# A two-block decoder kernel: three projections in products of 512 columns instead of 256

## The chip, the cores and the metric

The kernel runs on one core of one Trainium2 chip. The metric is the device time of one execution in microseconds, and the time of a kernel is the median over its runs. TensorE multiplies, VectorE, ScalarE and GpSimd work on tiles, SyncE issues the transfers of the weights; they meet over semaphores.

## The reference, cut to what matters

Two decoder blocks follow each other, each on 256 tokens of 2048 features. All of it is float32.

```python
# first block (three mixers, then)
merged = (sigmoid(g_a) * (y_a @ wb[:r_a]) + sigmoid(g_b) * (y_b @ wb[r_a:r_b])
          + sigmoid(g_c) * (y_c @ wb[r_b:]))
x = x + merged @ w_out                                  # the first output projection, "wout"
x = x + conv_ffn(rms_norm(x, ffn_norm), ffn_w_up, ffn_conv_w, ffn_conv_b, ffn_w_down)
x = rms_norm(x, final_norm)
# second block
z = rms_norm_2(x, mix_norm_gain) @ w_in
h = x + concatenate([pool_mixer(z...), mla(z...)]) @ w_out_2
xn = rms_norm_2(h, ffn_norm_gain)
q = (xn @ w_pq).reshape(B, S, 8, 2, 128)                # the query projection, "pq"
s1, s2 = q[..., 0, :] @ sub_k1.T, q[..., 1, :] @ sub_k2.T
# top 16 of each, top 16 of their sums, softmax: gates of 128 experts a token out of 16384
h = h + sum_k gelu(expert_u[idx] . xn) * gate * expert_v[idx]
gate = sigmoid(rms_norm_2(h, ple_norm_gain) @ w_ple_gate)   # the last gate, "pg"
h = h + gate * (p @ w_ple_proj)
```

## The kernel before, in words

**Layout.** Activations lie transposed: feature tile k (128 features) is a tile of 128 partitions by 256 tokens, and 16 such tiles, k = 0 to 15, make the 2048 features. Weights come as panels of 128 x 2048 (1 MB): panel n holds, for one tile of output features, the 16 blocks of 128 x 128 that meet the 16 input tiles. SyncE fills a ring of two slots with the panels in one fixed order, in four quarters of four blocks each (fill and refill, L587). A quarter of a split panel is refilled when its low part has been taken.

**Split products.** To keep float32 accuracy with the faster 32-bit matmul type, each operand is cut into a high and a low part. ScalarE writes the high part of each quarter of a panel into whi (high_quarter, L472), after TensorE has read the same quarter of the panel before it: the fourth quarter waits for panel_done. VectorE (quarters 1 and 3) and GpSimd (quarters 0 and 2) subtract and write the low part, wlo (rests, L485; rest_one, L568; rests_alone, L493). There is one whi and one wlo, so the preparation follows one quarter behind the products. Activations are split alike; high and low part of the normalised input lie side by side in xhl, and those of the merged tiles in mhl, each 16 tiles high and then 16 tiles low.

**Two forms of a block.** In the narrow form (project_split and products, L659 to L661) block k of a panel is three products of 256 columns: high weights by high input, high weights by low input, low weights by high input, all summed in one half of a bank of PSUM:

```python
                pe.matmul(out, whi[:, b], hi, start=start, stop=False, **kw)
                pe.matmul(out, whi[:, b], lo, start=False, stop=False, **kw)
                return pe.matmul(out, wlo[:, b], hi, start=False, stop=stop, **kw)
```

In the wide form (project_wide, L694 and L695) the high weights meet both input parts in one product of 512 columns, whose second half lands in the second half of the bank, and the low weights follow with 256 columns. Whoever reads the bank adds its halves. Before the change, the wide form stands in the feed-forward up projection (88 panels) and in the expert panels from number 36 on (92 panels); the narrow form in wout, in the second block's input projection, in wout2, pq, pg and the first 36 expert panels. The down projection and the expert outputs use a third form (L775 to L777).

**Evacuation.** Panel p goes to bank p mod 4 and waits until the panel four before has been evacuated (evac_done). The evacuation is VectorE's in all places that the change touches:

- wout: evac_add takes the rests of the next panel, waits for panel_done, and adds the bank to the residual (L1301 is the helper's line). ScalarE's high_and_squares waits for that, writes the high tile of the next input (tile_high, L546), after each fourth panel squares four tiles (L2152), and only then goes on to the high parts of the panel after next. VectorE writes the low tile (tile_low, L552). GpSimd folds the squares (fold, L562) between its rests. The first up panel reads the tiles as they come; in the second one TensorE sums the folded squares (folded_sums, L747), from which VectorE makes rstd (statistics: L1304 and the reciprocal L1318, with ScalarE's root between).
- pq: query(j) multiplies the bank by rstd into q2, normal(j) (L1307) writes tile j of the expert input. Panels 0 and 1 are evacuated only after the statistics, and no rest of VectorE is placed between them. After the last ones come the residual parts of the expert input (x_rest, L576) and query(15); the score products (L1251) wait for all 16 queries, ScalarE copies them out, and VectorE's top-16 code, the digits of the indices and GpSimd's 256 indirect transfers (L2768, the scatter of the gates) follow while TensorE does the expert panels.
- pg: gate(j) takes the rests of the next panel, waits for panel_done and multiplies the bank by rstd into gx; ScalarE (embed) applies the sigmoid and then makes the high parts of the panel after next; finish(j) multiplies with the projected embedding and adds to the residual. SyncE writes the output in four pieces as finish goes on.

The order on each engine is written out by hand; the class Count numbers the steps on a semaphore, link makes the engine wait for its own instruction, and enter and leave carry the count through loops. VectorE's add_residual and the last gate run as hardware loops of four panels a turn.

## Time and profile before

| | us |
|---|---|
| median of 3 runs | 3664.87 |
| lowest and highest | 3664.02, 3666.03 |
| the profiled execution, its own time | 3666.28 |
| its span | 3664.70 |
| granted TensorE clock, mean share of full speed | 0.992 |

The page gives busy times of each engine, the chain that ended last and the costliest groups. Where it ends, the timeline of an engine in a short stretch shows each instruction with its start, its length, and, in brackets, the idle time before it with the one that released it. Products overlap in the records: a product's length runs until its end is out of the array, while the next one has begun. wout runs from about 816 to 911 us, up from 911, pq from 2001 to 2097, the scores to 2110, pg from 3562 to 3659.

### The profile page before, as it was taken

How to read it: one execution, taken by the hardware profiler on the slowest of the kernel's cores; microseconds unless marked ns; L12 is line 12 of the kernel's file. 1: busy time of each engine (PE TensorE's matmuls, PEld its weight loads, DVE VectorE, ACT ScalarE, POOL GpSimd, SP SyncE). 2: the span in 40 equal slices, each digit the busy share in tenths (PEclk: the TensorE clock that was granted, in tenths of full speed). 3: DMA queues.
4: the chain of work that ended last, by engine and by line, in shares of the span. 5: the costliest groups of instructions: out<-in, count | busy, mean ns of one | idle time of the engine just before them, and what ended most of it. 6: DMA issues, size and time to landing. Idle time of an engine off the chain costs nothing.

```text
span 3664.7 us, 69606 instructions
## 1 busy us (share of the span) xinstructions
PE 3589.7 (98%) x21612; PEld 3174.8 (87%) x21612; DVE 2128.0 (58%) x3499; ACT 1771.0 (48%) x3033; POOL 1846.1 (50%) x1326
## 2 busy tenths in 40 slices
PE   8999999999999999998999999999999999999999
PEld 6889989999888888888869999988888888888889
DVE  6759764555777775336446597655555433333345
ACT  1134455545444444555335456554554555555554
POOL 0005665555555554444135483777776455555543
PEclk9999999999999999999999999999999999999999
DMA  5444444565677765664424555777777776776655
GB/s 175 144 142 154 155 152 135 175 201 179 210 231 231 232 198 181 193 193 136 132 94 160 174 185 183 184 186 187 187 185 183 228 215 218 218 216 215 217 187 166
DMA packets 388742, 672.38 MB, mean 183 GB/s; under 512 B 75968, under 2 KB 76096, under 8 KB 386064
## 3 DMA queue, kind: packets, MB, share of 16 engines
q1 hardware_dynamic: 344304, 630.48, 55.2%
q0 software_dynamic: 44320, 40.32, 5.2%
q8 instruction: 74, 1.21, 0.1%
q14 instruction: 44, 0.36, 0.0%
HBM read 649.53 MB, written 21.10 MB: 183 GB/s over the span
## 4 chain that ended last, share of the span: by engine, by line
PE 71%; POOL 13%; issue 6%; DVE 6%; ACT 2%; DMA 1%; SPq 0%; ACTq 0%; POOLq 0%; DVEq 0%; PEldq 0%
POOL gates L2768 11%; PE ps L694 9%; PE ps L775 8%; PE ps L776 8%; PE ps L777 8%; PE ps L659 8%; PE ps L661 7%; PE ps L660 7%; PE ps L648 5%; PE ps L695 4%; DVE arena L1301 2%; POOL wlo L493 1%; PE ps L1077 1%; DMA gates<-arena 1%; ACT arena L2152 1%
## 5 line engine op out<-in xcount | busy, mean ns | idle before, releaser
L472 ACT ACTIVATE whi<-ring 128x512 fp32r<-128x512 f32 x2180 | 1356.0, 631 | 1284.5 <-PE ps L661 441.9
L485 POOL TENSOR_TENSOR wlo<-ring,whi 128x512 fp32r<-128x512 f32 x714 | 964.3, 1352 | 1037.7 <-ACT whi L472 1037.1
L485 DVE TENSOR_TENSOR wlo<-ring,whi 128x512 fp32r<-128x512 f32 x702 | 568.8, 816 | 841.7 <-ACT whi L472 821.9
L694 PE MATMUL ps<-xhl,whi 128*128 128x512 f32 x2880 | 1019.2, 399 | 9.4 <-DVE wlo L493 6.6
L695 PE MATMUL ps<-xhl,wlo 128*128 128x256 f32 x2880 | 806.9, 280 | 0.0
L659 PE MATMUL ps<-xhl,whi 128*128 128x256 f32 x2320 | 666.3, 287 | 16.8 <-DVE wlo L485 4.7
L694 PEld LDWEIGHTS ps<-xhl,whi 128*128 128x128 f32 x2880 | 541.6, 188 | 147.5 <-DVE wlo L485 9.0
L660 PE MATMUL ps<-xhl,whi 128*128 128x256 f32 x2320 | 659.3, 284 | 0.0
L661 PE MATMUL ps<-xhl,wlo 128*128 128x256 f32 x2320 | 659.2, 284 | 0.0
L695 PEld LDWEIGHTS ps<-xhl,wlo 128*128 128x128 f32 x2880 | 544.3, 189 | 0.0
L775 PE MATMUL ps<-whi,xhl 128*128 128x512 f32 x1360 | 529.1, 389 | 0.0
L776 PE MATMUL ps<-wlo,xhl 128*128 128x512 f32 x1360 | 529.1, 389 | 0.0
L777 PE MATMUL ps<-whi,xhl 128*128 128x512 f32 x1360 | 529.1, 389 | 0.0
L2768 POOL DMA_INDIRECT gates<-arena x256 | 412.1, 1610 | 188.8 <-issue 93.4
L659 PEld LDWEIGHTS ps<-xhl,whi 128*128 128x128 f32 x2320 | 447.8, 193 | 21.8 <-issue 5.5
L660 PEld LDWEIGHTS ps<-xhl,whi 128*128 128x128 f32 x2320 | 448.1, 193 | 0.2
L661 PEld LDWEIGHTS ps<-xhl,wlo 128*128 128x128 f32 x2320 | 447.8, 193 | 0.0
L493 DVE TENSOR_TENSOR wlo<-ring,whi 128x512 fp32r<-128x512 f32 x384 | 258.2, 697 | 226.5 <-ACT whi L472 226.4
L775 PEld LDWEIGHTS ps<-whi,xhl 128*128 128x128 f32 x1360 | 255.3, 188 | 53.2 <-POOL wlo L485 0.2
L776 PEld LDWEIGHTS ps<-wlo,xhl 128*128 128x128 f32 x1360 | 255.3, 188 | 53.0
L777 PEld LDWEIGHTS ps<-whi,xhl 128*128 128x128 f32 x1360 | 255.3, 188 | 52.8
L493 POOL TENSOR_TENSOR wlo<-ring,whi 128x512 fp32r<-128x512 f32 x176 | 236.8, 1370 | 107.2 <-ACT whi L472 103.2
(259 smaller groups left out, 4096.7 us busy)
## 6 DMA issues: line engine op xcount, KB each, us to landing
ring<-stream SPq DMA_DIRECT2D x2380, 256.0 KB, 3.6
gates<-arena POOLq DMA_DIRECT2D x16, 1024.0 KB, 6.6
arena<-gates POOLq DMA_DIRECT2D x32, 512.0 KB, 6.3
gates<-arena POOLq DMA_INDIRECT x256
res<-xT SPq DMA_DIRECT2D x4, 512.0 KB, 8.1
res<-xT POOLq DMA_DIRECT2D x1, 2048.0 KB, 11.2
outT<-res POOLq DMA_DIRECT2D x1, 2048.0 KB, 9.6
parked<-outT POOLq DMA_DIRECT2D x1, 2048.0 KB, 11.1
```

The source lines that it names most:

```text
L472: act.activation(quarters(whi, g), quarters(ring[:, n % SLOTS, :], g), ACT.Copy).then_inc(w_hi, 1)
L485: eng.tensor_tensor(quarters(wlo, g), quarters(ring[:, n % SLOTS, :], g), quarters(whi, g).bitcast(F32), ALU.subtract).then_inc(done, 1)
L493: eng.tensor_tensor(quarters(wlo, g), quarters(ring[:, n % SLOTS, :], g), quarters(whi, g).bitcast(F32), ALU.subtract).then_inc((w_lo_pool ...
L659: pe.matmul(out, whi[:, b], hi, start=start, stop=False, **kw)
L660: pe.matmul(out, whi[:, b], lo, start=False, stop=False, **kw)
L661: return pe.matmul(out, wlo[:, b], hi, start=False, stop=stop, **kw)
L694: pe.matmul(ps[:, p % 4, :], whi[:, b], xhl[:, :, t], start=(k == 0), stop=False, skip_group_check=True)
L695: mm = pe.matmul(ps[:, p % 4, 0:T], wlo[:, b], xhi[:, t], start=False, stop=(k == KD - 1), skip_group_check=True)
L775: pe.matmul(ps[:, 4 * b + g, :], hi, whi[:, w], start=first, stop=False)
L776: pe.matmul(ps[:, 4 * b + g, :], hi, wlo[:, w], start=False, stop=False)
L777: mm = pe.matmul(ps[:, 4 * b + g, :], lo, whi[:, w], start=False, stop=end)
L2768: pool.indirect_dma_start(gates, bass.IndirectOffsetOnAxis(ap=place[:, c:c + 1], axis=0), weight[:, c:c + 1], None, compute_op=ALU.add).th ...
```

## The change

TensorE does wout, pq and pg in the wide form. project_wide gets the waits for the parts of its input and the choice of the input (xhl, or mhl for the merged tiles); residual_wide takes the place of split_residual, and wide_loop that of split_loop in pq and pg. VectorE brings the halves together: in wout by a second addition to the residual, in pq and pg by a reduction of the bank into half a free bank (6 and 5), which the multiplication by rstd then reads. The first addition and the reductions are steps of their own (L), so the counts of the loops change with them.

```diff
--- before.py
+++ after.py
@@ -681,18 +681,20 @@
                     if middle and g == 1:
                         middle()
 
-            def project_wide(n, p, i=None, tiles=None, middle=None):
+            def project_wide(n, p, i=None, tiles=None, middle=None, name=None, x=xhl):
 
 
                 pe.wait_ge(evac_done, turn(i, 4, p - 3))
                 for g in range(4):
                     quarter_ready(n, g, i, 4)
+                    if name:
+                        pe.wait_ge((x_lo_pool, x_lo_dve)[g % 2], XQ[name] // 2 + g // 2 + 1)
                     for k in range(4 * g, 4 * g + 4):
                         b, t = slice(k * P, (k + 1) * P), slice(k * T, (k + 1) * T)
                         if tiles:
                             pe.wait_ge(t_lo, TILES[tiles] + k + 1)
-                        pe.matmul(ps[:, p % 4, :], whi[:, b], xhl[:, :, t], start=(k == 0), stop=False, skip_group_check=True)
-                        mm = pe.matmul(ps[:, p % 4, 0:T], wlo[:, b], xhi[:, t], start=False, stop=(k == KD - 1),
+                        pe.matmul(ps[:, p % 4, :], whi[:, b], x[:, :, t], start=(k == 0), stop=False, skip_group_check=True)
+                        mm = pe.matmul(ps[:, p % 4, 0:T], wlo[:, b], x[:, 0, t], start=False, stop=(k == KD - 1),
                                        skip_group_check=True)
                     mm.then_inc(quarter_used if g < 3 else panel_done, 1)
                     if middle and g == 1:
@@ -747,14 +749,22 @@
                     mm = pe.matmul(ps[:, bank, 0:T], ones, sq[:, k * T:(k + 1) * T], start=(k == 0), stop=(k == 3))
                 mm.then_inc(rms_ss, 1)
 
-            def split_residual(n, p, name, r, sq):
-
-                x = parts_of(name)
+            def residual_wide(n, p, name, x):
+
                 for j in range(4):
-                    project_split(n + j, p + j, name if j == 0 else None, x=x)
+                    project_wide(n + j, p + j, name=name if j == 0 else None, x=x)
                 with pe.Fori(0, 3) as i:
                     for j in range(4, 8):
-                        project_split(n + j, p + j, None, i, x=x)
+                        project_wide(n + j, p + j, i, x=x)
+
+            def wide_loop(n, p, count):
+
+                turns = count // 4
+                with pe.Fori(0, turns) as i:
+                    for j in range(4):
+                        project_wide(n + j, p + j, i)
+                for j in range(4 * turns, count):
+                    project_wide(n + j, p + j)
 
             def accumulate_all(n, count, tiles_before, p_end, first_tile, last_read):
 
@@ -1036,7 +1046,7 @@
             with pe.Fori(0, 3) as i:
                 for m in range(4, 8):
                     merge(m, i)
-            split_residual(PANELS["wout"], OUT["wout"], "merged", 1, nx())
+            residual_wide(PANELS["wout"], OUT["wout"], "merged", mhl.rearrange("p (a t) -> p a t", a=2))
 
 
             project_wide(PANELS["up"], OUT["up"], tiles="ffn")
@@ -1236,9 +1246,9 @@
                     half_panel(j, g)
 
 
-            project_split(PANELS["pq"], OUT["pq"], None, tiles="ffn2")
-            project_split(PANELS["pq"] + 1, OUT["pq"] + 1, None, middle=lambda: folded_sums(6, sq_attn))
-            split_loop(PANELS["pq"] + 2, OUT["pq"] + 2, KD - 2)
+            project_wide(PANELS["pq"], OUT["pq"], tiles="ffn2")
+            project_wide(PANELS["pq"] + 1, OUT["pq"] + 1, middle=lambda: folded_sums(6, sq_attn))
+            wide_loop(PANELS["pq"] + 2, OUT["pq"] + 2, KD - 2)
             n = PANELS["subk"]
             arrive(n)
             for b in range(2):
@@ -1277,11 +1287,11 @@
                 mm.then_inc(panel_done, 1)
 
             pe.wait_ge(S["pp_ev"], 1)
-            project_split(PANELS["pg"], OUT["pg"], None, tiles="ple")
+            project_wide(PANELS["pg"], OUT["pg"], tiles="ple")
             pe.wait_ge(S["pp_ev"], 3)
-            project_split(PANELS["pg"] + 1, OUT["pg"] + 1, None, middle=lambda: folded_sums(7, nx()))
+            project_wide(PANELS["pg"] + 1, OUT["pg"] + 1, middle=lambda: folded_sums(7, nx()))
             pe.wait_ge(S["pp_ev"], 7)
-            split_loop(PANELS["pg"] + 2, OUT["pg"] + 2, KD - 2)
+            wide_loop(PANELS["pg"] + 2, OUT["pg"] + 2, KD - 2)
 
 
         @block.vector
@@ -1347,9 +1357,11 @@
                     one(j)
                 with dve.Fori(0, count // 4 - 1) as i:
                     evac.enter(i, 4)
+                    step.enter(i, 4)
                     for j in range(4, 8):
                         one(j, i)
                     evac.leave(count // 4 - 1)
+                    step.leave(count // 4 - 1)
                 tile_low(dve, name, count - 1)
 
             def evac_add(p, j, i=None):
@@ -1357,7 +1369,8 @@
                 rests(dve, n + 1, i, 4)
                 dve.wait_ge(panel_done, turn(i, 4, n + 1))
                 c = res[:, j * T:(j + 1) * T] if i is None else res[:, bass.ds(i * (4 * T) + j * T, T)]
-                evac.link(tt(c, c, ps[:, p % 4, 0:T], ALU.add))
+                L(tt(c, c, ps[:, p % 4, 0:T], ALU.add))
+                evac.link(tt(c, c, ps[:, p % 4, T:2 * T], ALU.add))
 
             def panel_of(p):
 
@@ -1938,10 +1951,15 @@
             statistics(6, meanwhile=lambda: rests(dve, PANELS["pq"] + 2))
             evac.base, evac.k = OUT["pq"], 0
 
+            def both_halves(out, bank):
+
+                return dve.tensor_reduce(out, ps[:, bank, :].rearrange("p (a t) -> p t a", a=2), AX.X, ALU.add)
+
             def query(j):
 
                 dve.wait_ge(panel_done, PANELS["pq"] + j + 1)
-                evac.link(tt(q2[:, j * T:(j + 1) * T], ps[:, (OUT["pq"] + j) % 4, 0:T], rstd[:], ALU.mult))
+                L(both_halves(ps[:, 6, 0:T], (OUT["pq"] + j) % 4))
+                evac.link(tt(q2[:, j * T:(j + 1) * T], ps[:, 6, 0:T], rstd[:], ALU.mult))
 
             def normal(k):
 
@@ -2105,7 +2123,8 @@
                 dve.wait_ge(panel_done, turn(i, 4, PANELS["pg"] + j + 1))
                 if j >= 2:
                     dve.wait_ge(S["gate_act"], turn(i, 4, j - 1))
-                evac.link(tt(gx[j % 2], ps[:, j % 4, 0:T], rstd[:], ALU.mult))
+                L(both_halves(ps[:, 5, 0:T], j % 4))
+                evac.link(tt(gx[j % 2], ps[:, 5, 0:T], rstd[:], ALU.mult))
 
             def finish(j, i=None):
 
@@ -2123,8 +2142,8 @@
                 gate(j)
                 finish(j - 1)
             with dve.Fori(0, KD // 4 - 2) as i:
-                for c in (step, evac, N["out_ready"]):
-                    c.enter(i, 4)
+                for c, per in ((step, 8), (evac, 4), (N["out_ready"], 4)):
+                    c.enter(i, per)
                 for j in range(4, 8):
                     gate(j, i)
                     finish(j - 1, i)
```

## Rows read from the trace of the kernel before

**Rows 1.** The page, part 1: busy time, share of the span and instructions of each engine.

```profile
PE 3589.7 (98%) x21612; PEld 3174.8 (87%) x21612; DVE 2128.0 (58%) x3499; ACT 1771.0 (48%) x3033; POOL 1846.1 (50%) x1326
```

**Rows 2.** The page, part 4: the chain that ended last, by engine and by line.

```profile
PE 71%; POOL 13%; issue 6%; DVE 6%; ACT 2%; DMA 1%; SPq 0%; ACTq 0%; POOLq 0%; DVEq 0%; PEldq 0%
POOL gates L2768 11%; PE ps L694 9%; PE ps L775 8%; PE ps L776 8%; PE ps L777 8%; PE ps L659 8%; PE ps L661 7%; PE ps L660 7%; PE ps L648 5%; PE ps L695 4%; DVE arena L1301 2%; POOL wlo L493 1%; PE ps L1077 1%; DMA gates<-arena 1%; ACT arena L2152 1%
```

**Rows 3.** Timeline of TensorE where the scatter ends: start, length, instruction, [idle, releaser].

```profile
2840.77 0.79 PE L694 MATMUL ps<-xhl,whi 128*128 128x512 f32 x1 [6.56 <-DVE wlo L493]
```

**Rows 4.** The page, part 5: groups of products, mean ns of one.

```profile
L694 PE MATMUL ps<-xhl,whi 128*128 128x512 f32 x2880 | 1019.2, 399 | 9.4 <-DVE wlo L493 6.6
...
L659 PE MATMUL ps<-xhl,whi 128*128 128x256 f32 x2320 | 666.3, 287 | 16.8 <-DVE wlo L485 4.7
```

**Rows 5.** Busy time by window, L659, then L694: stretch, length, PE busy (count), PEld, clock.

```profile
2024.00:2096.00 72.00, 56.60 (x200) 38.40 (x201) 1.00 0.64 188
...
2500.00:2700.00 200.00, 200.00 (x567) 106.36 (x566) 1.00 0.77 185
```

**Rows 6.** Timeline of the first output projection, panels 3 to 5.

```profile
841.68 0.41 DVE L1301 TENSOR_TENSOR res<-res,ps 128x256 f32<-128x256 f32 x1
...
844.33 1.67 ACT L472 ACTIVATE whi<-ring 128x512 fp32r<-128x512 f32 x3 [0.55 <-ACT arena L2152]
...
845.04 2.99 POOL L485 TENSOR_TENSOR wlo<-ring,whi 128x512 fp32r<-128x512 f32 x2 [4.07 <-ACT whi L472]
...
845.52 3.06 DVE L485 TENSOR_TENSOR wlo<-ring,whi 128x512 fp32r<-128x512 f32 x2 [2.90 <-ACT whi L472]
...
846.38 0.39 PE L659 MATMUL ps<-mhl,whi 128*128 128x256 f32 x1 [0.26 <-POOL wlo L485]
```

**Rows 7.** Groups of the up projection by form, 1000 to 1050 us.

```profile
L1701 DVE TENSOR_REDUCE ps<-ps 128x256 f32<-128x512 f32 x9 | 6.2, 686 | 0.0
```

**Rows 8.** Timeline of the hand-over from first output projection to up.

```profile
915.76 1.29 POOL L568 TENSOR_TENSOR wlo<-ring,whi 128x512 fp32r<-128x512 f32 x1 [3.76 <-ACT whi L472]
...
917.19 0.47 PE L694 MATMUL ps<-xhl,whi 128*128 128x512 f32 x1
```

**Rows 9.** Timeline of the first output projection, ahead of panel 10.

```profile
871.54 2.85 POOL L562 TENSOR_TENSOR arena<-arena 128x1024 f32<-128x1024 f32 x1
...
873.11 1.14 ACT L472 ACTIVATE whi<-ring 128x512 fp32r<-128x512 f32 x2
```

**Rows 10.** Timeline of the query projection, panels 1 to 3.

```profile
2008.51 0.36 PE L659 MATMUL ps<-xhl,whi 128*128 128x256 f32 x1 [0.82 <-POOL wlo L485]
...
2018.72 1.75 DVE L1318 RECIPROCAL rstd<-rstd 128x256 f32<-128x256 f32 x1 [1.04 <-ACT rstd L2152]
...
2022.81 1.28 DVE L485 TENSOR_TENSOR wlo<-ring,whi 128x512 fp32r<-128x512 f32 x2
...
2023.55 0.39 PE L659 MATMUL ps<-xhl,whi 128*128 128x256 f32 x1
```

**Rows 11.** Timeline where the query projection ends and the scores begin.

```profile
2099.86 0.35 PE L1251 MATMUL ps<-ring,arena 128*128 128x128 f32 x1 [2.62 <-DVE arena L1301]
```

**Rows 12.** Timeline of the last gate, panels 0 to 4.

```profile
3584.21 1.28 ACT L2152 ACT_TABLE_LOAD   x1
...
3587.84 2.19 ACT L472 ACTIVATE whi<-ring 128x512 fp32r<-128x512 f32 x4
...
3589.89 0.38 PE L659 MATMUL ps<-xhl,whi 128*128 128x256 f32 x1 [0.67 <-POOL wlo L485]
```

**Rows 13.** Timeline of the last gate's loop, ScalarE and GpSimd.

```profile
3609.79 1.18 ACT L472 ACTIVATE whi<-ring 128x512 fp32r<-128x512 f32 x2
...
3610.49 1.29 POOL L485 TENSOR_TENSOR wlo<-ring,whi 128x512 fp32r<-128x512 f32 x1 [2.48 <-ACT whi L472]
...
3615.96 1.15 ACT L472 ACTIVATE whi<-ring 128x512 fp32r<-128x512 f32 x2 [0.53 <-ACT arena L2152]
```

**Rows 14.** Timeline of VectorE, its last evacuation.

```profile
3659.34 0.43 DVE L1301 TENSOR_TENSOR arena<-ps,rstd 128x256 f32<-128x256 f32 x1 [3.14 <-PE ps L661]
```

## Prediction

> **What bounds the kernel now.** I read the page's engine table first, then the chain that ended last, then the costliest groups, then panels in order of time. TensorE is busy 98% of the span [rows 1], and the chain runs through its products for most of the time, except for 11% on GpSimd's scatter of the gates [rows 2]. That scatter is started by VectorE after the query projection and ends in a TensorE wait of 6.56 us [rows 3]; work before it and after it adds up in one line, so a stage's shift is a shift of the end. One panel is 16 blocks k. A block is three products of 256 columns in the narrow form and one of 512 plus one of 256 in the wide form. The busy sums of the groups (287 ns and 399 ns a product [rows 4]) overlap and must not be added: they would promise 176 ns a block. What counts is how many blocks go by. In a narrow stretch without a wait 200 blocks take 72 us, 0.360 us each; in a wide stretch 567 take 200 us, 0.353 us each [rows 5]. Both forms push 768 columns through a block, which is why the two are so near.
>
> **Products, 48 panels.** The change takes 768 blocks from 0.360 to 0.353 us. That is 0.007 us a block, 0.112 us a panel and 5.4 us in all if TensorE never waited. It waits, so below each stage is followed to the point where something else sets its pace.
>
> The Trainium skill (TensorE: Matmul & The Clock Gate, Back-to-back issue gap) gives a warm gap of N/2.4 ns plus about 2.5 ns a product. By it one product fewer a block would save 2.5 ns, 1.9 us in all, an estimate; the rows show nearly three times that, and the sum goes by the rows. The same section also names a sustained 131 ns for products of 512 columns; rows 5 leave no room for it, since a wide block would then be far shorter than 0.353 us.
>
> **VectorE, new work.** In the first output projection evac_add becomes two linked additions. One takes 0.41 us [rows 6]; with the link the second costs 0.45 us. In the other two stages a reduction from 512 to 256 goes ahead of the multiplication: the feed-forward stage has this very operation at 0.686 us [rows 7], with the link 0.73 us. VectorE has room for both, since it is busy 58% of the span [rows 1]. So the new work costs nothing where nobody waits for the evacuation soon. The bound is 0.45 or 0.73 us for each place where somebody does, and zero elsewhere. The places:
>
> **First output projection (wout).** Each fourth panel, ScalarE squares four tiles after the evacuation before it makes the high parts of the panel after next. The chain is addition at 841.68, high tile and squares, high parts at 844.33, GpSimd's rest at 845.04, restart of TensorE at 846.38 after a wait [rows 6]. There is no slack in it, so the second addition goes in whole. This occurs at panels 5, 9 and 13 of the stage and once more in the hand-over to the first up panel, where GpSimd's rest at 915.76 releases the product at 917.19 [rows 8]. Ahead of panels 10 and 14 a fold on GpSimd from 871.54 to 874.39 holds its next rest, while the first of two high parts (873.11, 1.14 for both) is ready about 0.65 us sooner [rows 9]; 0.45 us more is hidden there, but what TensorE gains in panels 9 and 13 is lost. Sum: panel 0 gives three quarters (its second quarter waits for VectorE), 0.084, and panels 1 to 3 0.336; then +0.45 leaves +0.03. Panels 5 to 7 give 0.336, +0.45: +0.14. Panels 10 and 11 give 0.224, +0.45: +0.37. Panels 14 and 15 give 0.224, +0.45: **+0.6 us** for the stage. In the other panels GpSimd's rest is ready about 1.2 us before it is needed, and 0.45 + 0.11 fits.
>
> **Query projection (pq).** Panel 0 gains nothing, since panel 1 starts behind a GpSimd rest that TensorE does not drive (2008.51) [rows 10]. Then comes a knot: after the reciprocal (2018.72) VectorE does query 0, normal 0, query 1, normal 1, and only at 2022.81 the rest that panel 3's second quarter waits for; TensorE restarts at 2023.55 [rows 10]. Both queries get 0.73 us longer, +1.46, less the 0.112 of panel 1 that the reciprocal follows: +1.35. From there 12.75 panels without a wait give back 1.43. At the tail VectorE goes from query 14 over normals and residual parts to query 15 without a pause, and the score products wait 2.62 us for it, until 2099.86 [rows 11]. Both are longer again, +1.46, from a TensorE that is at +0.03 at the end of panel 14: **+1.5 us**. TopK, the scatter and the expert panels all start from there and shift alike.
>
> **Last gate (pg).** Panels 0 and 1 are held by folds and squares that do not depend on products. The evacuations 0 and 1 run ahead of and under ScalarE's table load, which ends at 3585.49 and which the first sigmoid waits for [rows 12], so their 1.46 us are hidden: if that cover were gone they would cost at most that. Gate 2 is not: it leads to the sigmoid, the high parts at 3587.84 and TensorE's restart at 3589.89 [rows 12]. +0.73 less 0.056: +0.67. Twelve panels give 1.34. In each of them the same chain is there with slack: high parts at 3609.79 and GpSimd's rest at 3610.49 for 1.29 us [rows 13], ready at 3611.78, while panel 8, four panels of 5.76 us after the restart, begins at 3613.0. 1.2 us less 0.73 and 0.11 leaves 0.35. I take one wait of 0.35 at panel 5, which follows the late gate 3, and 0.3 at the loop's turn, where ScalarE idles 0.53 us before the high parts at 3615.96 [rows 13]. At the end the last evacuation (3659.34) has only the final additions behind it [rows 14]: +0.73. Sum **+0.7 us**. SyncE's queue and the transfers see the same releases, a little earlier or later, and nothing new is queued on them or on GpSimd.
>
> **Sum.** 0.6 + 1.5 + 0.7 = +2.8 us. The profiled execution took 3666.28 us (span 3664.70), 1.41 us above the median of 3664.87; against its own time the sum gives 3669.1, against the median **3667.7 us**. A measurement here can tell about 0.2% from no change, 7.3 us, so this is no change, on the slower side.
>
> **Rivals.** (1) The covers are better than I think: queries and gates hide and the whole 5.4 us stays, 3659.5. For it: TensorE's 98%. Against it: the waits of [rows 10 to 12], which end on VectorE's work. (2) The change does not shorten the products, because a block costs the same where its operands come from the merged tiles or because the wide pace belongs to its own stage. Then the waits alone count: 4 x 0.45 in wout, 4 x 0.73 in pq, 2 x 0.73 and 0.35 in pg, 6.5 us, 3671.4. By the rule of 2.5 ns of the Trainium skill named above the time would lie between, at about 3670. (3) Slower: the loop evacuation, sigmoid or high tile, high parts, GpSimd's rest, becomes the pace of the stages. It decides once its slack is below the 0.84 us that reduction and faster panels take; the slack I read is 1.2 in pg. If contention between VectorE's and GpSimd's rests eats 0.8 of it, each of 12 panels loses 0.45, 5.4 us on top of the sum, 3673.1. For it: two rests of VectorE beside two of GpSimd took 3.06 us [rows 6], and 1.28 us where GpSimd was idle [rows 10]. Against it: the addition that reads PSUM at 841.68 [rows 6] took 0.41 us, and the loop has kept 1.2 us in each panel shown. (4) All small terms cancel, 3664.9.
>
> **How the numbers follow.** Forecast 0.57, (1) 0.12, (2) 0.13, (3) 0.12, (4) 0.06. The forecast's own band is 3665 to 3670.5, as the waits of 0.35 and 0.3 in pg may be 0 or double, and so may one of the four in wout or pq. The range goes from 3662 to 3673: it leaves out (1) and half of (3), 0.18. Faster by over 0.2% (under 3657.5) needs more than the whole saving: 0.03. Slower by over 0.2% (over 3672.2) is most of (3) and the upper edge of (2): 0.11. Same: 0.86.
>
> **What the profile of after would show.** The three stages without products of L659 to L661, and 0.353 us a block in them; if it is 0.360, (2) holds. In wout four waits for GpSimd's rest, each some 0.55 us longer than 0.26. In pq the restart after the reciprocal 1.4 us later against the reciprocal, and a wait ahead of the scores of some 4 us instead of 2.62. In pg steady panels without a wait for GpSimd's rest; if every panel has one, (3) holds. At the end 0.73 us more from the last product to the last output. If the score products wait no longer than now, the pq term is wrong; that is the largest one.

## The result, and the profile after

Over 8 runs the changed kernel takes 3677.41 us in the median (3673.69 to 3682.84), beside 3665.24 us (3661.45 to 3669.23) for the kernel before: ratio 1.0035, 95% interval 1.0025 to 1.0045, or 9 to 16 us. It is slower, and above the range of the prediction. The profiled execution took 3678.9 us, its span is 3677.3 us.

The page of the kernel after: engine table and three of the costliest groups.

```profile
PE 3592.0 (98%) x20844; PEld 3136.5 (85%) x20844; DVE 2178.4 (59%) x3547; ACT 1767.8 (48%) x3033; POOL 1853.6 (50%) x1326
...
L485 POOL TENSOR_TENSOR wlo<-ring,whi 128x512 fp32r<-128x512 f32 x714 | 972.0, 1364 | 1039.4 <-ACT whi L472 1038.8
L696 PE MATMUL ps<-xhl,whi 128*128 128x512 f32 x3392 | 1204.9, 400 | 17.0 <-DVE wlo L493 6.6
L485 DVE TENSOR_TENSOR wlo<-ring,whi 128x512 fp32r<-128x512 f32 x702 | 585.5, 840 | 802.5 <-ACT whi L472 782.1
```

The product count fell by 768, as the change says [rows 1, 4]. TensorE's idle time ahead of wide products is 17.0 us where it was 9.4, while ahead of narrow ones it only fell from 16.8 to 14.7. One group should not have moved: the rests L485. The same 702 rests of VectorE take 840 ns in the mean. Before they took 816, so 17 us of busy time are new in an instruction that nobody changed.

**Where the time went.** Four lengths are read from TensorE's timeline, each from mark to mark: *wout* from the restart in panel 0 to the second up panel, *pq* from the start of its panel 1 to the first score product, *pg* from the restart behind the sums of squares to the last product, *end* from there to VectorE's last end. All in us:

| kernel | wout | pq | pg | end | ratio to before |
|---|---|---|---|---|---|
| before | 98.67 | 91.35 | 84.48 | 2.63 | |
| after | 101.05 | 95.12 | 87.58 | 3.36 | 1.0035 (1.0025 to 1.0045) |
| e1 | 100.93 | 90.28 | 84.51 | 2.64 | 1.0000 (0.9991 to 1.0010) |
| e2 | 98.66 | 94.27 | 84.49 | 2.63 | 1.0008 (0.9998 to 1.0018) |
| e3 | 98.68 | 91.22 | 87.42 | 3.38 | 1.0013 (1.0004 to 1.0023) |
| e4 | 97.15 | 88.57 | 82.92 | 2.64 | 0.9978 (0.9969 to 0.9988) |
| e5 | 102.76 | 96.60 | 87.97 | 3.38 | 1.0041 (1.0027 to 1.0055) |
| e6 | 99.23 | 91.35 | 85.34 | 3.10 | 1.0003 (0.9993 to 1.0013) |
| e7 | 98.68 | 88.96 | 84.49 | 2.65 | 0.9994 (0.9985 to 1.0003) |
| e8 | 98.69 | 88.29 | 84.49 | 2.65 | 0.9986 (0.9977 to 0.9995) |
| e9 | 95.10 | 87.35 | 81.68 | 3.37 | 0.9979 (0.9970 to 0.9988) |
| e10 | 97.13 | 88.95 | 83.63 | 2.64 | 0.9989 (0.9980 to 0.9998) |

One execution of e6 took 7156 us and is in no ratio. A stage that a kernel leaves alone repeats to 0.04 us in wout and pg. In pq e1 stands 1.1 below its like; the reason is in VectorE's rows ahead of the scores, before and e1:

```profile
2097.09 2.29 DVE L576 TENSOR_TENSOR xhl<-arena,xhl 128x1024 fp32r<-128x1024 f32 x1
...
2099.80 1.22 DVE L576 TENSOR_TENSOR xhl<-arena,xhl 128x1024 fp32r<-128x1024 f32 x1
```

Before, this residual part begins inside a rest of GpSimd (2096.67 to 2098.30) and takes 2.29 us. In e1 a high quarter of ScalarE came late, behind a transfer (2099.22, idle 0.44), GpSimd's rest began after the residual part (2099.93), and the part took 1.22 us; the scores then waited 1.54 us instead of 2.62.

After against before the four lengths give 2.38 + 3.77 + 3.10 + 0.73 = **+10.0 us**; the stretches between the stages are equal to 0.4 us. Another 2.3 us are there when wout starts (820.80 instead of 818.52), ahead of any changed code; over all twelve traces that mark lies between 815.9 and 821.1, so I count it as variation. The stretches between the stages vary too from kernel to kernel, though nothing in them is changed: 1089.5 to 1093.0 us from wout to pq, 1472.2 to 1475.3 from pq to pg. So a shift of 2 or 3 us is read from the stages and not from the whole; of the 12.2 us between the two medians about 2 stay without a place.

**First output projection.** Timeline around the end of panel 3; columns as in the rows of before. First three rows of the kernel before that my prediction did not use (ScalarE, VectorE, GpSimd), then VectorE, ScalarE, GpSimd and TensorE in the kernel after.

```profile
840.41 0.63 ACT L472 ACTIVATE whi<-ring 128x512 fp32r<-128x512 f32 x1 [0.81 <-PE ps L661]
...
841.07 0.69 DVE L485 TENSOR_TENSOR wlo<-ring,whi 128x512 fp32r<-128x512 f32 x1 [1.55 <-ACT whi L472]
...
839.68 1.30 POOL L485 TENSOR_TENSOR wlo<-ring,whi 128x512 fp32r<-128x512 f32 x1 [0.70 <-ACT whi L472]
```

```profile
840.61 1.38 DVE L485 TENSOR_TENSOR wlo<-ring,whi 128x512 fp32r<-128x512 f32 x1 [1.29 <-ACT whi L472]
842.57 1.12 DVE L485 TENSOR_TENSOR wlo<-ring,whi 128x512 fp32r<-128x512 f32 x1 [0.58 <-ACT whi L472]
843.61 0.86 DVE L1311 TENSOR_TENSOR res<-res,ps 128x256 f32<-128x256 f32 x2
...
841.91 0.63 ACT L472 ACTIVATE whi<-ring 128x512 fp32r<-128x512 f32 x1 [0.76 <-PE ps L697]
844.71 0.51 ACT L546 ACTIVATE xhl<-res,par  x1 [2.17 <-DVE res L1311]
846.72 2.19 ACT L472 ACTIVATE whi<-ring 128x512 fp32r<-128x512 f32 x4 [0.55 <-ACT arena L2171]
...
840.13 3.01 POOL L485 TENSOR_TENSOR wlo<-ring,whi 128x512 fp32r<-128x512 f32 x2 [2.67 <-ACT whi L472]
847.42 2.96 POOL L485 TENSOR_TENSOR wlo<-ring,whi 128x512 fp32r<-128x512 f32 x2 [4.28 <-ACT whi L472]
...
848.74 0.50 PE L696 MATMUL ps<-mhl,whi 128*128 128x512 f32 x1 [1.32 <-POOL wlo L485]
```

The two additions together take 0.86 us, +0.45 as predicted. But they start 1.70 us after the fourth high quarter begins (843.61 less 841.91); before it was 1.27 (840.41 to 841.68). The rest between them took 0.69 us before and takes 1.12 now: GpSimd, which had ended its second rest at 840.98, now works a pair from 840.13 to 843.14, across it. So from that high quarter to TensorE's restart it is 6.83 us instead of 5.97, +0.86: 0.45 for the addition, 0.43 for the meeting of the rests. The wait is 1.32 instead of 0.26. It recurs at panels 9, 13 and at the hand-over.

**Query projection.** Timeline behind the reciprocal, and TensorE's restart in panel 3, kernel after.

```profile
2023.57 1.75 DVE L1328 RECIPROCAL rstd<-rstd 128x256 f32<-128x256 f32 x1 [1.04 <-ACT rstd L2171]
2025.36 0.70 DVE L1956 TENSOR_REDUCE ps<-ps 128x256 f32<-128x512 f32 x1
...
2027.48 0.69 DVE L1956 TENSOR_REDUCE ps<-ps 128x256 f32<-128x512 f32 x1
...
2029.06 2.35 DVE L485 TENSOR_TENSOR wlo<-ring,whi 128x512 fp32r<-128x512 f32 x2
...
2028.75 1.51 POOL L485 TENSOR_TENSOR wlo<-ring,whi 128x512 fp32r<-128x512 f32 x1 [1.48 <-ACT whi L472]
...
2030.87 0.50 PE L696 MATMUL ps<-xhl,whi 128*128 128x512 f32 x1 [2.86 <-DVE wlo L485]
```

The first rest starts 5.49 us after the reciprocal does, where it was 4.09: +1.40, the two reductions. Then the pair takes 2.35 us, not 1.28 [rows 10], since at 2028.75 GpSimd has begun a rest of its own; TensorE gets its quarter another 1.07 us later. And behind that wait came something that the kernel before did not have at this place. Busy time by window, of L696: length, PE busy (count), PEld, granted clock, DMA share, GB/s.

```profile
2024.00:2031.00 7.00, 4.03 (x13) 2.12 (x12) 1.00 0.62 189
2031.00:2035.00 4.00, 3.94 (x8) 2.03 (x8) 0.57 0.65 192
2035.00:2104.00 69.00, 69.00 (x197) 36.68 (x196) 1.00 0.63 183
```

From 2035 on a block takes 0.353 us at the full clock (2.4 GHz), by the starts of its products. In the 4 us ahead of it the granted clock was 0.57, which is most of the time at 1.2 GHz (0.50 from 2032 to 2034): six blocks from 2031.32 to 2034.97 took 3.65 us instead of 2.12, so about 1.5 us were lost. At the end of the stage the scores wait as foretold, 3.94 us:

```profile
2108.68 0.68 PE L1261 MATMUL ps<-ring,arena 128*128 128x128 f32 x4 [3.94 <-DVE arena L1311]
```

**Last gate.** First two rows of the kernel before that my prediction did not use, from GpSimd's and VectorE's timelines; then one turn of the loop in the kernel after.

```profile
3612.48 1.29 POOL L485 TENSOR_TENSOR wlo<-ring,whi 128x512 fp32r<-128x512 f32 x1 [0.70 <-ACT whi L472]
...
3613.88 0.69 DVE L485 TENSOR_TENSOR wlo<-ring,whi 128x512 fp32r<-128x512 f32 x1 [1.54 <-ACT whi L472]
```

```profile
3609.22 1.68 ACT L472 ACTIVATE whi<-ring 128x512 fp32r<-128x512 f32 x3
...
3614.66 0.42 ACT L2171 ACTIVATE arena<-arena 128x256 f32<-128x256 f32 x1 [2.85 <-DVE arena L1311]
...
3609.93 3.00 POOL L485 TENSOR_TENSOR wlo<-ring,whi 128x512 fp32r<-128x512 f32 x2 [2.97 <-ACT whi L472]
...
3610.41 3.07 DVE L485 TENSOR_TENSOR wlo<-ring,whi 128x512 fp32r<-128x512 f32 x2 [0.60 <-ACT whi L472]
3613.40 0.69 DVE L1956 TENSOR_REDUCE ps<-ps 128x256 f32<-128x512 f32 x1
...
3617.32 0.50 PE L696 MATMUL ps<-xhl,whi 128*128 128x512 f32 x1 [0.22 <-POOL wlo L485]
```

Before, GpSimd's second rest ended at 3613.77 and VectorE's began at 3613.88: 0.1 us apart, and VectorE's took its 0.69. After, three high quarters come in one go behind the late sigmoid, each engine has its two rests back to back, and the rests of the two engines meet: 3.07 us for VectorE's two. The reduction waits for the second of them and the next sigmoid for it. That is a closed loop, and it is TensorE's pace: of eleven panels behind the restart eight take 5.95 to 6.07 us, one 6.38 and the last two 5.89 and 5.81, where sixteen blocks of 0.353 make 5.65.

### The profile page after: what moved, and what is told of

It reads as the page before. It is cut to its first block, busy times and chain, and to the rows that moved or that the text cites. A ratio compares the mean times of both kernels' runs of the same rounds, so it can differ in the third digit from the quotient of the medians.

```text
span 3677.3 us, 68138 instructions
## 1 busy us (share of the span) xinstructions
PE 3592.0 (98%) x20844; PEld 3136.5 (85%) x20844; DVE 2178.4 (59%) x3547; ACT 1767.8 (48%) x3033; POOL 1853.6 (50%) x1326
## 4 chain that ended last, share of the span: by engine, by line
PE 69%; POOL 14%; issue 6%; DVE 6%; ACT 2%; DMA 1%; ACTq 0%; POOLq 0%; DVEq 0%
PE ps L696 12%; POOL gates L2787 11%; PE ps L785 8%; PE ps L786 8%; PE ps L787 8%; PE ps L697 6%; PE ps L659 6%; PE ps L661 5%; PE ps L660 5%; PE ps L648 5%; DVE arena L1311 2%; POOL wlo L485 1%; POOL wlo L493 1%; PE ps L1087 1%; DMA gates<-arena 1%
## 5 line engine op out<-in xcount | busy, mean ns | idle before, releaser
L485 POOL TENSOR_TENSOR wlo<-ring,whi 128x512 fp32r<-128x512 f32 x714 | 972.0, 1364 | 1039.4 <-ACT whi L472 1038.8
L696 PE MATMUL ps<-xhl,whi 128*128 128x512 f32 x3392 | 1204.9, 400 | 17.0 <-DVE wlo L493 6.6
L485 DVE TENSOR_TENSOR wlo<-ring,whi 128x512 fp32r<-128x512 f32 x702 | 585.5, 840 | 802.5 <-ACT whi L472 782.1
L696 PEld LDWEIGHTS ps<-xhl,whi 128*128 128x128 f32 x3392 | 638.4, 188 | 183.0 <-DVE wlo L485 10.9
L659 PE MATMUL ps<-xhl,whi 128*128 128x256 f32 x1808 | 520.2, 288 | 14.7 <-DVE wlo L485 4.7
L660 PE MATMUL ps<-xhl,whi 128*128 128x256 f32 x1808 | 514.2, 284 | 0.0
L493 DVE TENSOR_TENSOR wlo<-ring,whi 128x512 fp32r<-128x512 f32 x384 | 258.3, 697 | 226.5 <-ACT whi L472 226.4
L659 PEld LDWEIGHTS ps<-xhl,whi 128*128 128x128 f32 x1808 | 349.8, 193 | 18.7 <-DVE wlo L485 4.9
L660 PEld LDWEIGHTS ps<-xhl,whi 128*128 128x128 f32 x1808 | 349.9, 194 | 0.1
```

The source lines that it names most:

```text
L485: eng.tensor_tensor(quarters(wlo, g), quarters(ring[:, n % SLOTS, :], g), quarters(whi, g).bitcast(F32), ALU.subtract).then_inc(done, 1)
L493: eng.tensor_tensor(quarters(wlo, g), quarters(ring[:, n % SLOTS, :], g), quarters(whi, g).bitcast(F32), ALU.subtract).then_inc((w_lo_pool ...
L696: pe.matmul(ps[:, p % 4, :], whi[:, b], x[:, :, t], start=(k == 0), stop=False, skip_group_check=True)
```

## The experiments

**e1, e2, e3: one stage each.** Only wout, only pq, only pg in the new form with its VectorE work; the other two as before. The edits in short:

```text
 e1:  residual_wide(PANELS["wout"], ...)      pq, pg: project_split, split_loop
 e2:  project_wide / wide_loop for "pq"       wout, pg: project_split
 e3:  project_wide / wide_loop for "pg"       wout, pq: project_split
```

> Wide products and the second addition in the first output projection alone. Stage lengths are read from the trace: wout from TensorE's restart in panel 0 to the second panel of up took 98.7 us before and 101.1 with the whole change. Delay theory (the evacuation comes later, its followers come later, and the rests of GpSimd and VectorE then meet): wout again about 101.1, the other stages as before, and the whole about 2.4 us over before. Rival (the stages act on each other, the first one alone costs nothing): wout near 98.7.

> Wide products and the reduction in the query projection alone. From the start of panel 1 to the first score product it took 91.4 us before, 95.1 with the whole change. Delay theory: about 95.1 again, with the wait of 3 us at panel 3, a stretch at half clock behind it and a wait of about 4 us ahead of the scores; the whole about 3.8 us over before. Rival: without the first stage's change the half-clock stretch does not come, and it takes some 93.5.

> Wide products and the reduction in the last gate alone. From the restart behind the sums of squares to the last product it took 84.5 us before and 87.6 with the whole change, and from the last product to VectorE's last end 2.6 and 3.4. Delay theory: 87.6 and 3.4 again, the whole about 3.8 us over before, and in the loop each pair of GpSimd's rests takes 3.0 us. Rival: part of it was variation between executions, and it comes out under 86.

wout alone takes 100.93 (+2.26 of 2.38), pg alone 87.42 + 3.38 (+3.7 of 3.8): these two carry their own loss. pq alone takes 94.27, +2.9 of 3.8, halfway between the two expectations. Its waits and the slow stretch are there; what is missing is the pace of the blocks, 0.347 us in e2 and 0.353 in the kernel after (last section), 1.3 us over twelve panels. The whole of e1 did not move (1.0000, where +2.4 us was expected); in its trace pq is 1.1 us shorter, as said above, and the unchanged stretches together 2.2. In e2 the restart after the knot again has a long wait, and the clock falls behind it, to 0.50 from 2022 to 2025 (windows of all of TensorE: length, busy, clock, DMA share, GB/s):

```profile
2021.54 0.50 PE L696 MATMUL ps<-xhl,whi 128*128 128x512 f32 x1 [2.80 <-DVE wlo L485]
```

```profile
2020.00:2024.00 4.00, 2.46 (x9) 0.75 0.23 70
2024.00:2028.00 4.00, 4.00 (x21) 0.82 0.74 251
```

**e4: wide products, one read.** All three stages wide, but VectorE reads only the first half of each bank, as before. So the product of high weights and low input is left out of these three projections.

```diff
-                L(tt(c, c, ps[:, p % 4, 0:T], ALU.add))
-                evac.link(tt(c, c, ps[:, p % 4, T:2 * T], ALU.add))
+                evac.link(tt(c, c, ps[:, p % 4, 0:T], ALU.add))
```

> The wide products in all three stages, but VectorE reads only the first half of the bank, as before: the product of the high weights with the low part of the input is left out of the result. This is the change without VectorE's new work. Delay theory: the products alone save their 0.007 us a block and the waits stay those of before: wout about 97.5 us, pq about 90, pg about 83.3, the whole 3 to 5 us under before. Rival (the wide products themselves disturb the preparation of the weights): the rests of GpSimd take 3.0 us a pair and the stages stay as long as with the change, 101.1, 95.1 and 87.6.

The lengths fall by 1.5, 2.8 and 1.6, 5.9 us in all, and the whole by 0.22%. The products do save about what was foretold (5.4), and the loss comes with VectorE's second read: from e4 to the kernel after it is 3.9 + 6.6 + 4.7 + 0.7 = 15.8 us. Some 1.3 us of the 15.8, and of the 5.9, are the pace of e4's blocks in pq, 0.347 us, and not shown to be VectorE's. Rival (2) falls.

**e5: narrow products, delayed evacuation.** The reverse: narrow products, with an operation of the same length put ahead of each evacuation.

```diff
+                L(dve.tensor_copy(ps[:, 6, 0:T], ps[:, p % 4, 0:T]))
+                evac.link(tt(c, c, ps[:, 6, 0:T], ALU.add))      # wout
+                L(same(ps[:, 6, 0:T], (OUT["pq"] + j) % 4))      # pq; pg alike
```

> The reverse of the run before it: narrow products everywhere, as before the change, but VectorE does an operation of the new work's length ahead of each evacuation (a copy of the bank in the first output projection, a maximum over each element twice in the other two, so that the result is the same). Delay theory: the time comes from the later evacuations alone, so the stages are as long as with the change or longer: wout 100.5 to 102, pq 95 to 96.5, pg 87 to 89, end 3.4; the half-clock stretch behind panel 3 of pq is there too. Rival (wide products are needed for the loss): wout 98.7, pq 91.4 to 93, pg 84.5.

102.76, 96.60 and 87.97, and 3.38 at the end: 13.6 us over before without one wide product added, more than the 10.0 of the change and most of the 15.8 from e4. GpSimd's rests are paired here too, and the wait in the knot is 2.76 us. Timeline of GpSimd in the gate loop, of TensorE in the query projection, kernel e5.

```profile
3613.79 2.99 POOL L485 TENSOR_TENSOR wlo<-ring,whi 128x512 fp32r<-128x512 f32 x2 [2.97 <-ACT whi L472]
...
2033.65 0.38 PE L659 MATMUL ps<-xhl,whi 128*128 128x256 f32 x1 [2.76 <-DVE wlo L485]
```

**e6: less of it.** wout wide, but each fourth panel narrow with one addition; pg narrow with a copy of 0.42 us instead of the reduction of 0.69.

```diff
+                if j % 4 < 3:  ... two additions
+                else:          evac.link(tt(c, c, ps[:, p % 4, 0:T], ALU.add))
+                L(dve.tensor_copy(ps[:, 5, 0:T], ps[:, j % 4, 0:T]))      # pg
```

> Two separate places. First output projection: wide as in the change, but the panel ahead of each squaring (3, 7, 11 and 15 of the stage) stays narrow with one addition. Delay theory: the waits of 1.6 us at panels 5, 9 and 13 fall back to some 0.6 and wout takes about 98; rival (the loop is slow anyway because the rests meet): it stays over 100. Query projection as before. Last gate: narrow, with a copy of 0.42 us ahead of each evacuation instead of the reduction of 0.69. Delay theory: VectorE's and GpSimd's rests do not yet meet, so pg stays within 0.5 us of 84.5; the rival says that any delay counts in each panel, which would be 12 x 0.45 us, over 89.

99.23 and 85.34, between the two expectations. In wout the fourth panel's evacuation is short again, and still the restarts came 0.82 to 1.08 us behind the product before them (0.53 before, 1.6 after), and GpSimd's rests are a pair (839.84, 3.00 us): the late evacuations of the other panels are enough for that. Here my own theory of one waiting panel in four was too local. In pg the 0.42 us cost 0.46 us at the restart and 0.40 over the panels after it. GpSimd's two rests are a pair of 3.00 us in each panel there too, and the loop still runs at 5.76 to 5.86 us in all but one panel. So meeting rests with this smaller delay cost TensorE little; the loss of the change needs both, large enough to use up the slack.

**e7, e8: another order in pq.** VectorE does panel 3's second quarter before query 0 and its fourth before query 2, and query 15 ahead of the last residual parts; e7 in the narrow form, e8 wide.

```diff
+            rest_one(dve, PANELS["pq"] + 3, 1)
             for j in range(KD - 1):
-                if j > 1:
+                if j == 2:
+                    rest_one(dve, PANELS["pq"] + 3, 3)
+                elif j > 2:
                     rests(dve, PANELS["pq"] + j + 1)
 ...
             x_rest(dve, "eu", nx(), 0)
+            query(KD - 1)
             rest_one(dve, PANELS["eu"], 1)
             x_rest(dve, "eu", nx(), 1)
-            query(KD - 1)
```

> The kernel before with another order on VectorE at the two ends of the query projection: the rest of panel 3's second quarter goes ahead of query 0, and query 15 goes ahead of the rest and the residual part in front of it. No wide product. Delay theory: the restart of panel 3 no longer waits, and the wait of 2.6 us ahead of the scores falls under 1: pq takes 88 to 89.5 instead of 91.4 us. The whole is 1 to 3 us under before, which five rounds can hardly tell.

> The same order with wide products and the reduction in the query projection alone. Delay theory: the wait of 3 us, the half-clock stretch behind it and most of the wait of 4.2 us are gone, so that the shorter blocks show: pq takes 87 to 88 us, about 1 us under the same order with narrow products and 7 under the change's 95.1. Rival (the reduction costs in each panel): 92 or more.

88.96 and 88.29. The wide stage is 6.0 us shorter than in e2 by an order alone, although its blocks go at 0.353 us here and at 0.347 there. Timeline of TensorE, kernel e8: at the knot and at the scores.

```profile
2026.19 0.50 PE L696 MATMUL ps<-xhl,whi 128*128 128x512 f32 x1 [0.21 <-DVE wlo L568]
...
2097.05 0.57 PE L1262 MATMUL ps<-ring,arena 128*128 128x128 f32 x3 [1.34 <-DVE arena L1312]
```

With 0.21 us of wait in place of 2.80 the granted clock stays at 1.00 (2022 to 2084).

**e9, e10: the loop cut.** Beside the order of e7, ScalarE makes the first two high quarters of the panel after next *before* the high tile or sigmoid that waits for the evacuation. e9 is the whole change with this, e10 has narrow products throughout.

```diff
                     for j in range(4):
-                        high_parts(act, n + j, i, 4)
+                        for m, g in ((j, 2), (j, 3), (j + 1, 0), (j + 1, 1)):
+                            high_quarter(act, n + m, g, i, 4)
                         act.wait_ge(evac_done, i * 4 + (p + j + 1))
                         tile_high(act, name, j, i)
```

> The whole change, all three stages wide with VectorE's two reads, and three orders changed: (a) ScalarE makes the high quarters 0 and 1 of the panel after next ahead of the panel's high tile or sigmoid, in the first output projection and the last gate, so that these parts no longer wait for VectorE's evacuation; (b) the order of the rests in the query projection as in the run that changed it alone; (c) the last query ahead of the other work at its end. Theory (the loss is a loop: late evacuation, late high parts, rests of GpSimd and VectorE bunched, late evacuation): the first output projection takes 96 to 97.5 us instead of 101.05, the query projection about 88.3 instead of 95.1, the last gate 82.5 to 84 instead of 87.6, the end 3.4; the whole 3657 to 3660 us, 0.15 to 0.25% under the kernel before. Rival (the rests of the two engines meet in any order, and the added VectorE work is paid in full): the first output projection stays over 100 us and the last gate over 87; the whole is no better than 3669 us.

> The same three orders with the narrow products and one addition of before in all three stages, so none of the change. Theory: first output projection about 97 us (98.67 before), query projection about 89.0 (91.35 before), last gate about 84 (84.48), end 2.6; the whole about 0.1% under the kernel before. The difference to the wide run tells what the wide products are worth once the loop is cut: the theory wants the wide one 0 to 3 us faster. Rival: the order does nothing for the outer two stages when they are narrow (98.6 and 84.5), and the wide one is slower than this by 6 us or more.

e9 takes 3657.35 us (3665.41 for before in the same runs) and beats both kernels: 0.9979. Its wide stages are now shorter than e4's, which left the additions out; in pg that is 1.2 us, and the pace alone makes it (0.347 us a block in e9, 0.353 in e4). The rival, that the rests meet in any order, falls. Timeline of one turn of the gate loop, kernel e9, then a group of its page.

```profile
3602.54 0.63 ACT L472 ACTIVATE whi<-ring 128x512 fp32r<-128x512 f32 x1 [0.75 <-PE ps L697]
3603.93 0.63 ACT L472 ACTIVATE whi<-ring 128x512 fp32r<-128x512 f32 x1 [0.76 <-PE ps L697]
3604.46 0.40 ACT L2174 ACTIVATE arena<-arena 128x256 f32<-128x256 f32 x1
3605.31 0.63 ACT L472 ACTIVATE whi<-ring 128x512 fp32r<-128x512 f32 x1 [0.45 <-PE ps L697]
...
3603.25 1.30 POOL L485 TENSOR_TENSOR wlo<-ring,whi 128x512 fp32r<-128x512 f32 x1 [1.45 <-ACT whi L472]
3606.02 1.64 POOL L485 TENSOR_TENSOR wlo<-ring,whi 128x512 fp32r<-128x512 f32 x1 [1.48 <-ACT whi L472]
...
3603.80 1.02 DVE L1311 TENSOR_TENSOR arena<-arena 128x256 f32 x1 [0.23 <-DVE arena L1311]
```

```profile
L485 DVE TENSOR_TENSOR wlo<-ring,whi 128x512 fp32r<-128x512 f32 x700 | 552.2, 795 | 800.6 <-ACT whi L472 779.1
```

ScalarE's high quarters are released by TensorE, evenly, 1.39 us apart; the sigmoid stands between them and holds nobody. The rests come one at a time, and VectorE's mean is 795 ns, below that of before (816). Some meetings remain (1.02 and 1.64) but they fall where there is room. In the gate loop by itself (groups of VectorE, 3590 to 3655 us; before, after, e9) a rest takes 1050, 1493 and 701 ns:

```profile
L485 DVE TENSOR_TENSOR wlo<-ring,whi 128x512 fp32r<-128x512 f32 x24 | 25.1, 1050 | 25.5 <-ACT whi L472 25.5
...
L485 DVE TENSOR_TENSOR wlo<-ring,whi 128x512 fp32r<-128x512 f32 x20 | 29.7, 1493 | 8.3 <-ACT whi L472 8.0
...
L485 DVE TENSOR_TENSOR wlo<-ring,whi 128x512 fp32r<-128x512 f32 x19 | 13.3, 701 | 13.1 <-ACT whi L472 11.8 <-DVE res L1311 0.6
```

e10 stands at 0.9989. By the lengths it gains 4.8 us on before and e9 9.6: half of e9's gain belongs to the orders and not to the wide products. Between e9 and e10 the lengths differ by 2.03 + 1.60 + 1.95 − 0.73 = 4.9 us. The medians differ by 3.4 us, about as much as each interval reaches to either side, so the whole alone would not show it.

## Why the prediction was wrong

- **Products, 5.4 us: right, with some luck.** e4 gave 5.9. A wide block has two paces at the full clock, 0.353 us (forecast, and found in pq after) and 0.347 (pq of e4, 1.3 us of the 5.9); the rows before showed only the first in a long stretch, and which one comes was not foreseen. The Trainium skill's rule of 2.5 ns a product (TensorE: Matmul & The Clock Gate, Back-to-back issue gap) would have given 1.9; the measurement decides for the rows.
- **VectorE's price, 0.45 and 0.73 us: right** in each single place (843.61, 2025.36), as was the +0.73 at the end (3.36 less 2.63) and the longer wait at the scores (3.94 instead of 2.62).
- **wout, forecast +0.6, measured +2.4: the step that failed** is the price of "the second addition goes in whole", 0.45 us at each of four places. The waits grew by 1.06 us, where 0.45 + 0.11 had been counted: 4 x 0.5 us too little. The missing 0.43 is the rest in front of the additions, 1.12 instead of 0.69.
- **pq, forecast +1.5, measured +3.8.** Both queries and the tail came as priced (+1.40, and 1.3 at the scores). Missing were 1.07 us, the pair of rests at 2.35 instead of 1.28, and 1.5 us at the lower clock: 1.5 + 2.6 = 4.1, and the two priced places together gave 0.2 less than priced. The step that failed is the 1.35 us of the knot: it moved the rests later with their old duration and gave the longer wait behind them no price in the clock. I had noted that a pair takes 1.28 us "where GpSimd was idle", and not asked whether it would be idle 1.4 us later.
- **pg, forecast 0 without the end, measured +3.1: the step that failed** is "1.2 us less 0.73 and 0.11 leaves 0.35", with the rest ready at 3611.78 and panel 8 at 3613.0. That is the slack of the first quarter with all durations kept. Between GpSimd's second rest and VectorE's second there was 0.1 us, and the delay closes it; the evacuation, which stands behind VectorE's second rest, is then late by more than the reduction. TensorE waited ahead of every panel. Rival (3) named this mechanism and its size (0.45 us a panel, where 0.3 to 0.4 was found), and I gave it 0.12 on the ground that the loop had kept its 1.2 us in each panel, the very number that did not count.
- **Sum.** In wout and pq the places of the waits were right and their sizes off; in pg the loop became the pace, which the forecast had ruled out. In all three durations were taken from rows of a spacing that the change itself removes.

That the wait and the late evacuation cause each other is shown by e5 (delay alone, more than the whole loss) against e9 (same delay, loop cut, no loss). How much of the loop's cost is pure delay and how much the longer rests was read from rows, not separated by a run; e6 shows only that the longer rests with a smaller delay cost little. The fall of the clock in the knot comes with the long wait in all kernels that have one (after, e2, e5) and is gone with it (e8); no run changed one without the other.

## What to carry to other kernels

Before a delay is called hidden, look at the tightest gap between the two engines that work on the same kind of operand, not at the slack of the item that is needed first. Where an engine's prefetch stands in program order behind a wait for another engine's result, work added to that result is a loop, and its cost is paid in each turn; here moving the prefetch ahead of the wait, with a better order at the two ends of the query projection, was worth as much as the wide products, and turned their loss into a gain. A duration from the trace holds for the spacing at which it was taken.

## What the runs showed of the hardware

**Rests of two engines.** A rest of VectorE takes 0.69 us alone. Begun at 3611.00 in the kernel before, while GpSimd was in its rest of 3610.49, it took 1.34, and GpSimd's kept its 1.29 [rows 13].

```profile
3611.00 1.34 DVE L485 TENSOR_TENSOR wlo<-ring,whi 128x512 fp32r<-128x512 f32 x1 [0.65 <-ACT whi L472]
```

In the kernel after, all four of a panel take 3.55 us together (3609.93 to 3613.48), where each by itself would make 2 x 1.29 + 2 x 0.69 = 3.96 one after the other. The Trainium skill (SBUF — State Buffer, SBUF: two separate sides) calls the pair of ports that the two engines share an exclusive lock: an instruction of VectorE with two inputs in SBUF waits for the whole of a GpSimd instruction that began first. The trace agrees for one pair to 0.13 us (the later rest ended at 3612.34, by the rule at 3611.78 + 0.69), and the earlier one is not slowed; the four come within 0.4 us of a row one after the other. By that rule, an estimate from the starts in the rows above, VectorE's rest would wait 0.57 us in wout (842.57 to 843.14) and 0.98 in the knot (2029.06 to 2030.04), where 0.43 and 1.07 were measured.

**The clock.** After waits of 2.8 us in the middle of dense work (2030.87, and 2021.54 in e2) TensorE's granted clock read 0.57 (2031 to 2035) and 0.75 and 0.82 (2020 to 2028), part of the time at 1.2 GHz. Behind the scatter's wait of 6.56 us [rows 3] the kernel before reads 0.50 as well (2840 to 2844). After waits of 1.3 us in wout it did not (1.00 from 860 to 900). In between it went either way ahead of the scores: behind 2.62 us the kernel before reads 0.50 (2102 to 2104), behind 2.71 us e4 reads 1.00 (2096 to 2100). In the knot a wait that grew by 2.5 us cost nearly 4.

**Two paces of a wide block.** A narrow block took 0.360 us in wout, pq and pg wherever TensorE did not wait, in every kernel. A wide one took 0.353 or 0.347 us, both at a granted clock of 1.00. First products of a panel in the query projection, kernel after, eleven panels apart, then e2, ten panels apart:

```profile
2040.99 0.40 PE L696 MATMUL ps<-xhl,whi 128*128 128x512 f32 x1
...
2103.16 0.40 PE L696 MATMUL ps<-xhl,whi 128*128 128x512 f32 x1
```

```profile
2031.88 0.39 PE L696 MATMUL ps<-xhl,whi 128*128 128x512 f32 x1
...
2087.35 0.39 PE L696 MATMUL ps<-xhl,whi 128*128 128x512 f32 x1
```

That is 62.17 / 176 = 0.3532 and 55.47 / 160 = 0.3467. In pq e8 also has the first pace, e4 and e9 the second; in pg e4 has the first and e9 the second. Behind the knot's wait after went from the second pace to the first, e2 from the first to the second; no run shows what chooses it. So a wide block saves 0.007 or 0.013 us, and two wide kernels can differ by 1.3 us in a stage for this alone.
